# First gate and up weights interleaved by k tile, a row factor by an all-ones product, and one weight unit landing in a place of its own

## The chip, the cores and the metric

The kernel runs on one core of one Trainium2 chip. The metric is device time in microseconds of one execution. Before the change, three runs took 1002.99 to 1003.37 us, median 1003.11.

## The reference

One hybrid decoder layer on 512 tokens of width 1024, in float32: a half-step SwiGLU FFN, a mixer of three head groups (gated DeltaNet, block-sparse attention, cross-attention into 256 memory tokens), and a second half-step FFN. The part that the change touches:

```python
def rms_norm(x, gain, eps=1e-6):
    return x * rsqrt(mean(x * x, axis=-1) + eps) * gain

def swiglu_ffn(x, gain, w_gate, w_up, w_down):          # D_MODEL 1024, D_FF 2816
    h = rms_norm(x, gain)
    return (silu(h @ w_gate) * (h @ w_up)) @ w_down

x = x + 0.5 * swiglu_ffn(x, ffn1_norm, ffn1_w_gate, ffn1_w_up, ffn1_w_down)
...
k, v = split(rms_norm(mem, mem_norm) @ w_mem_kv)        # the memory products, 256 tokens
```

## The kernel before

Activations lie transposed: 128 partitions by 8 k tiles by 512 tokens. Each float32 operand is split into a high part (a rounded copy, type fp32r) and a low part (the remainder), and each product is three matmuls: high by high, high by low, low by high (`split_product`, L1916). A weight unit is 128 x 2048 values (1 MB): SyncE (SP) issues its transfer into one of two `raw` places, ScalarE (ACT) copies the high part into a ring of three `whi` places, and GpSimd (POOL) or VectorE (DVE) subtracts to make `wlo`. TensorE (PE) uses a unit when its low part is done. All queues are written out by hand, instruction by instruction, and tied by semaphores; no scheduler reorders them.

The row factor r = rsqrt(mean of squares) isn't applied to x ahead of the first products. They run on x times the gain, and `gate_scale` (L1241) multiplies the gate tile by r afterwards; `hidden` then multiplies SiLU(gate) by r once more (L1249) and by the up tile (L1253).

The program opens so. SP brings unit 0 (first 256 gate columns, all 8 k tiles) and x in four pieces each, two k tiles at a time (`PIECES`), then unit 1 (the up columns), the memory tokens, unit 2 and 3 (`w_mem_kv`) and the constants. PE runs 28 products on zeros (L2092), then `first_pair` for unit 0 (banks 0 and 1) and for unit 1 (banks 2 and 3), then `x_stats(0)` (sums of squares as four one-column products, L1930), then `mem_keys_values`, with `x_spread(0)` (L1947, the factor spread over the partitions by four small products) after its second k tile. On DVE, `x_stat` makes the sums, computes the factor on 128 x 4 values, and copies the spread factor to `rbc` (L1143). After that come `gate_scale`, `ablo` (L1371), the sums of the memory squares (`mem_sums`, L1199 to L1201), the `cv` copies and a reduction (L1376, L1377), and the first hidden tiles. `normalize` (L1269) and two sums for the later fast products (`t_total`, L1287) follow, then the first residual additions (`ffn_add`, L1363).

PE's second gate and up units (units 4 and 5, with POOL's first low parts, L485) follow the memory products, and then the first down unit (unit 6). PE may overwrite the up bank with unit 5's product only when DVE has made the first hidden tile (`h_done`), and the fifth output tile of the down unit only when DVE has added the first to x (`x_added`).

Stage 2, the norm ahead of the second FFN, already has another way, `x_stat_wide`: a product with an all-ones matrix leaves the sum of squares in every partition, and DVE computes the factor on 128 x 512 values.

Of the kernel before, what the change touches and what calls it, by code (L numbers as in the profile page):

```python
# [11 lines left out]
P = 128  # L12
# [15 lines left out]
U_FIRST, U_MEM = 0, 2  # L28
PIECES = [0, 2, 4, 6, 8]
NP = len(PIECES) - 1  # L30
U_IN = 10
# [37 lines left out]
def build(nc, stream, fast_stream, x_in, mem_in, ab_in, small_in, const_in, out):  # L69
    with ExitStack() as ctx:  # L70
# [96 lines left out]
        gbuf, _, nxt = place("gbuf", [P, 2, T], at=mid)  # L167
        hhi, _, nxt = place("hhi", [P, 4, T], F32R, at=nxt)
# [17 lines left out]
        sum2_hi, sum2_lo, ones_r = (place(f"sum2_{i}", [P, T], F32R, at=nxt2 - (KD - i) * T * 4)[0] for i in (1, 2, 7))  # L186
# [74 lines left out]

        def raw_of(f, g):

            return raw_down[f][:] if g == 2 else raw[:, g, :]
# [28 lines left out]
        def gcol(n, h, c):  # L293
# [3 lines left out]
        cst_in, masks_in, small_sem, ab_sem, out_done = (  # L297
            sem(n) for n in ("cst_in", "masks_in", "small_sem", "ab_sem", "out_done"))
        mem_sems = [sem(f"mem_in{i}") for i in range(2)]
        w0_in = [sem(f"w0_in{i}") for i in range(NP - 1)]  # L300
        half_in = [sem(f"half_in{i}") for i in range(3)]
# [84 lines left out]

        def in_bank(q):

            return q % 4 if q < 12 else q % 2 if q < 23 else 1
# [17 lines left out]
        def _(sp):  # L407
            def part(u, c0, c1, done):
                sp.dma_start(raw[:, u % RAW, c0:c1], stream[u:u + 1, :, c0:c1].rearrange("o p n -> (o p) n")
                             ).then_inc(done, 16)  # L410

            sp.dma_start(small[:], small_in).then_inc(small_sem, 16)
            for i in range(NP):
                k0, k1 = PIECES[i], PIECES[i + 1]
                part(0, 256 * k0, 256 * k1, w0_in[i] if i < NP - 1 else raw_in[0])
                sp.dma_start(x[:, k0:k1, :], x_in[:, k0:k1, :]).then_inc(x_sem[i], 16)
            part(1, 0, 1024, half_in[0])
            part(1, 1024, 2048, raw_in[1])
# [3 lines left out]
            part(2, 0, 1024, half_in[1])  # L422
# [4 lines left out]
            part(3, 0, 1024, half_in[2])  # L427
# [4 lines left out]
            def unit(u):  # L432
                sp.dma_start(raw[:, u % RAW, :], stream[u:u + 1, :, :].rearrange("o p n -> (o p) n")
                             ).then_inc(raw_in[u % RAW], 16)
# [24 lines left out]

            for u in range(EARLY, U_IN):  # L460
                sp.wait_ge(w_lo, u + 1 - RAW)
                unit(u)
# [15 lines left out]
        def _(pool):  # L478
            def split(u):
# [3 lines left out]
                for c0 in range(0, 2048, 2048 // parts):  # L483
                    c1 = c0 + 2048 // parts
                    ins = nc.gpsimd.tensor_tensor(wlo[:, u % RING, c0:c1], raw[:, u % RAW, c0:c1],  # L485
# [56 lines left out]
            pool.wait_ge(masks_in, 16)  # L542
# [26 lines left out]
        def _(act):  # L569
            A = nc.scalar  # L570

            def weight_hi(u):
# [8 lines left out]
                A.activation(whi[:, u % RING, :], raw[:, u % RAW, :], ACT.Copy).then_inc(w_hi, 1)  # L581

            def sqrt(n, width, c0=0):

                act.wait_ge(mean_ready, n + 1)
                A.activation(root[:, c0:c0 + width], msq_[:, c0:c0 + width], ACT.Sqrt).then_inc(root_ready, 1)

# [10 lines left out]
            def part_hi(u, c0, c1, landed, count, done):  # L598
                act.wait_ge(landed, count)
                A.activation(whi[:, u % RING, c0:c1], raw[:, u % RAW, c0:c1], ACT.Copy).then_inc(done, 1)  # L600
# [7 lines left out]
            for i in range(NP):  # L608
                k0, k1 = PIECES[i], PIECES[i + 1]
                if i < NP - 1:  # L610
                    part_hi(0, 256 * k0, 256 * k1, w0_in[i], 16, piece_hi)
                else:
                    part_hi(0, 256 * k0, 256 * k1, raw_in[0], 16, w_hi)
# [3 lines left out]
                for d in range(k0, k1):  # L617
                    x_high(0, S_G1, d)
            part_hi(1, 0, 1024, half_in[0], 16, piece_hi)
            part_hi(1, 1024, 2048, raw_in[1], 16, w_hi)  # L620
            A.activation(gain_qk[:, 0:1], col(S_MQ), ACT.Copy, scale=col(S_MK)).then_inc(gain_ready, 1)
            A.activation(gain_qk[:, 1:2], col(S_CQ), ACT.Copy, scale=col(S_CK)).then_inc(gain_ready, 1)
            for d in range(KD):
                x_square(0, d)
# [4 lines left out]
            part_hi(2, 0, 1024, half_in[1], 16, piece_hi)  # L629
            part_hi(2, 1024, 2048, raw_in[0], 32, w_hi)  # L630
            act.wait_ge(w_used, 1)
# [2202 lines left out]
```

## Time and profile before

| | us |
|---|---|
| median of three runs | 1003.11 |
| the profiled execution | 1002.87 |
| its span | 1001.1 |
| TensorE (PE) busy | 994.9 (99%) |
| VectorE (DVE) busy | 688.7 (69%) |
| GpSimd (POOL) busy | 505.1 (50%) |
| ScalarE (ACT) busy | 440.0 (44%) |

The chain of work that ended last is PE for 92% of the span, half of it the 128 x 512 products of L1916. Busy matmul time is modelled, and matmuls overlap, so the spacing of their starts tells more than their length. Times below are counted from the start of the span. In a timeline a row gives start, length (of the whole group, where it has a count), engine, line, operation, output from inputs, form, count, and in brackets the engine's idle time just before and what ended it.

### The profile page before, as it was taken

The numbers are of one execution on the slowest core, as the hardware profiler recorded it, in microseconds if no ns is written. First come the engines' busy times: TensorE is split into PE (matmuls) and PEld (weight loads), VectorE is DVE, ScalarE is ACT, GpSimd is POOL, SyncE is SP. The second block draws the span as 40 slices with busy tenths as digits, with TensorE's granted clock in tenths as the row PEclk, the third lists the DMA queues.
The fourth block names the chain that finished last, engine by engine and source line by source line (L and its number), as shares of the span: only waits on it lengthen the run. The fifth ranks groups of instructions, "written<-read, shape, count | busy, mean of one in ns | idle before, by whom it ended". The sixth has DMA issues, their size and how long they took to land.

```text
span 1001.1 us, 16467 instructions
## 1 busy us (share of the span) xinstructions
PE 994.9 (99%) x6826; PEld 876.2 (88%) x6826; DVE 688.7 (69%) x1084; ACT 440.0 (44%) x645; POOL 505.1 (50%) x289
## 2 busy tenths in 40 slices
PE   9999999999999999999999999999999999999998
PEld 7888999999999988788878788888899999999997
DVE  5896986766666486863547883687688776667745
ACT  7542543344433462444356664534244244443341
POOL 0364866667566433543252201635576675756741
PEclk9999999999999999999999999999999999999999
DMA  8332223331233212321221001223302332123312
GB/s 331 127 127 84 85 84 127 127 126 51 82 121 127 99 71 85 122 89 43 85 69 61 2 3 43 95 89 112 126 32 96 127 127 104 65 85 127 127 43 84
DMA packets 15770, 95.32 MB, mean 95 GB/s; under 512 B 2000, under 2 KB 2128, under 8 KB 5456
## 3 DMA queue, kind: packets, MB, share of 16 engines
q1 hardware_dynamic: 15696, 94.27, 26.4%
q8 instruction: 54, 0.88, 0.4%
q14 instruction: 20, 0.16, 0.0%
HBM read 92.16 MB, written 2.10 MB: 94 GB/s over the span
## 4 chain that ended last, share of the span: by engine, by line
PE 92%; DVE 3%; DMA 1%; ACT 1%; POOL 1%; SPq 0%; issue 0%; DVEq 0%; POOLq 0%
PE bank L1916 50%; PE bank L2044 32%; DMA raw<-stream 1%; POOL wlo L485 1%; PE bank L2336 1%; PE bank L2340 1%; PE bank L2450 1%; PE bank L2384 1%; PE bank L2362 1%; PE bank L2422 0%; PE bank L2439 0%; ACT sqx L606 0%; PE bank L2406 0%; PE bank L2396 0%; ACT whi L581 0%
## 5 line engine op out<-in xcount | busy, mean ns | idle before, releaser
L485 POOL TENSOR_TENSOR wlo<-raw,whi 128x1024 fp32r<-128x1024 f32 (+1 forms) x44 | 148.3, 3387 | 215.2 <-ACT whi L581 198.4
L2044 PE MATMUL bank<-t_ffn_hi,wlo 128*128 128x256 f32 x896 | 253.6, 283 | 0.0
L2044 PE MATMUL bank<-t_ffn_lo,whi 128*128 128x256 f32 x896 | 253.6, 283 | 0.0
L2044 PE MATMUL bank<-t_ffn_hi,whi 128*128 128x256 f32 x896 | 253.5, 283 | 0.0
L502 POOL TENSOR_TENSOR wlo<-sums,whi 128x512 fp32r<-128x512 f32 x128 | 170.4, 1354 | 120.3 <-ACT whi L695 120.1
L502 POOL TENSOR_TENSOR wlo<-raw,whi 128x512 fp32r<-128x512 f32 x96 | 158.7, 1667 | 39.3 <-ACT whi L695 39.3
L2044 PEld LDWEIGHTS bank<-t_ffn_lo,whi 128*128 128x128 f32 x896 | 172.0, 192 | 0.6
L2044 PEld LDWEIGHTS bank<-t_ffn_hi,whi 128*128 128x128 f32 x896 | 172.0, 192 | 0.6
L1916 PE MATMUL bank<-ahi,whi 128*128 128x512 f32 x432 | 171.2, 396 | 1.0 <-POOL wlo L485 1.0
L2044 PEld LDWEIGHTS bank<-t_ffn_hi,wlo 128*128 128x128 f32 x896 | 172.0, 192 | 0.0
L1916 PE MATMUL bank<-ahi,wlo 128*128 128x512 f32 x432 | 168.4, 390 | 0.0
L1916 PE MATMUL bank<-alo,whi 128*128 128x512 f32 x432 | 168.2, 389 | 0.0
L1363 DVE SCALAR_TENSOR_TENSOR x<-bank,x 128x512 f32<-128x512 f32 x176 | 117.1, 685 | 45.3 <-PE bank L1916 45.2
L1916 PE MATMUL bank<-hhi,whi 128*128 128x512 f32 x352 | 137.1, 390 | 0.0
L1916 PE MATMUL bank<-hlo,whi 128*128 128x512 f32 x352 | 137.1, 390 | 0.0
L1916 PE MATMUL bank<-hhi,wlo 128*128 128x512 f32 x352 | 136.9, 389 | 0.0
L695 ACT ACTIVATE whi<-sums 128x512 fp32r<-128x512 f32 (+2 forms) x72 | 68.4, 961 | 89.4 <-DVE sums L1308 65.6
L1916 PEld LDWEIGHTS bank<-ahi,whi 128*128 128x128 f32 x432 | 81.1, 188 | 20.8 <-POOL wlo L485 1.9
L1916 PEld LDWEIGHTS bank<-ahi,wlo 128*128 128x128 f32 x432 | 81.1, 188 | 17.4
L1916 PEld LDWEIGHTS bank<-alo,whi 128*128 128x128 f32 x432 | 81.2, 188 | 15.9
L695 ACT ACTIVATE whi<-raw 128x512 fp32r<-128x512 f32 (+1 forms) x64 | 54.0, 844 | 82.8 <-PE bank L2044 50.9
L1916 PEld LDWEIGHTS bank<-hhi,wlo 128*128 128x128 f32 x352 | 66.1, 188 | 13.8
(312 smaller groups left out, 1408.2 us busy)
## 6 DMA issues: line engine op xcount, KB each, us to landing
raw<-fast_in SPq DMA_DIRECT2D x32, 1024.0 KB, 4.9
raw<-stream SPq DMA_DIRECT2D x30, 1024.0 KB, 4.9
raw_down<-fast_in SPq DMA_DIRECT2D x18, 1024.0 KB, 7.0
raw<-stream SPq DMA_DIRECT2D x6, 512.0 KB, 6.3
x<-x_in SPq DMA_DIRECT2D x4, 512.0 KB, 6.9
out<-x SPq DMA_DIRECT2D x8, 256.0 KB, 2.0
raw<-stream SPq DMA_DIRECT2D x4, 256.0 KB, 6.1
memx<-mem_in SPq DMA_DIRECT2D x2, 512.0 KB, 10.6
```

The costliest lines, as they stand in the source:

```text
L485: ins = nc.gpsimd.tensor_tensor(wlo[:, u % RING, c0:c1], raw[:, u % RAW, c0:c1], whi[:, u % RING, c0:c1].bitcast(F32), ALU.subtract)
L502: nc.gpsimd.tensor_tensor(in_ring(wlo, ring_at, n), whole[:, PIECE * at:PIECE * (at + 1)], in_ring(whi, ring_at, n).bitcast(F32), ALU.subt ...
L695: A.activation(in_ring(whi, ring_at, m), whole[:, c0:c0 + m], ACT.Copy).then_inc(f_hi, m // PIECE)
L1363: V.scalar_tensor_tensor(out=x[:, d, :], in0=psum[4 + d % 4][:], scalar=0.5, in1=x[:, d, :], op0=ALU.mult, op1=ALU.add).then_inc(x_added, 1)
L1916: ins = E.matmul(dst, a, b, start=(n == 0 and i == 0), stop=(n == last and i == 2))
L2044: ins = E.matmul(psum[bank][:, HALF * h:HALF * (h + 1)], a, b[:, k, :], start=start and k == 0 and m == 0, stop=k == K2 - 1 and m == 2, sk ...
L2336: E.matmul(psum[Y_BANKS[r]][half[e], y_out(j, q)], bm[pair][half[r], j, 2 * q + e, :], x[half[r], j, 2 * q + e, :], start=True, stop=True)
L2340: i = E.transpose(psum[T_BANK][:, M * j + P * q:M * j + P * q + P], x[:, j, 2 * q:2 * q + 2, :].rearrange("p h t -> p (h t)"), ident)
L2362: i = E.matmul(psum[Y_BANKS[e]][half[r], s_out(j, q)], ty[pair][half[e], j, turned(q, r)], ty[pair][half[e], j, product(q, r)], start=True ...
L2384: E.matmul(psum[SCORE_BANKS[e]][:, 0:M], cq[half[e], t, cs], ck[half[e], t, :], start=True, stop=True).then_inc(s_ps, 1)
L2450: i = E.matmul(psum[TURN_BANKS[0]][half[e], 0:P], mv[:, b, v:v + DH], ptr[p % 2][:, e, b, :], start=(b == 0), stop=(b == n - 1))
```

## The change

- **Opening.** Units 0 and 1 are laid out anew on the host: each holds four k tiles, with 256 gate and 256 up columns for each (`both`, `PAIR`). Pieces are now of 1, 1, 2, 2 and 2 k tiles, weights and x in turn. `first_pair` runs k tile by k tile over all four banks. 16 products on zeros stand ahead of it instead of 28. ACT squares x between the pieces.
- **Row factor.** Stage 0 uses `x_stat_wide`, with places of its own for the sums. The all-ones product (`x_sums`, two matmuls of 512 columns) stands ahead of the fifth k tile of the memory products; the four one-column products and the four spreading products go. DVE makes unit 2's and 3's low parts ahead of the last sum. As `x_stat_wide` leaves another value in the bank, `ffn(0)` copies `rbc` there, as `ffn(1)` did.
- **First gate bank.** ACT copies the first two gate tiles out of banks 0 and 1 (`gate_out`), `gate_scale` reads those copies, and PE's second gate unit waits for the copies instead of for `gate_scale`.
- **Unit 4.** It lands in `raw_gate`, over the place of `hhi`, and its transfer waits for unit 2's high part (before: for unit 2's low part). ACT's first `hhi` copy waits until POOL has read it. The last table transfers share one semaphore and stand behind unit 4 on SP.

```diff
-PIECES = [0, 2, 4, 6, 8]
+PIECES = [0, 1, 2, 4, 6, 8]
...
+        raw_gate, _, _ = place("raw_gate", [P, 2048], at=nxt)
...
+        def raw_unit(u):
+            return raw_gate[:] if u == EARLY else raw[:, u % RAW, :]
... (SP)
-            sp.dma_start(abr[:], ab_in).then_inc(ab_sem, 16)
-            sp.dma_start(cst[:, C_LEV:C_SEL], const_in[:, C_LEV:C_SEL]).then_inc(masks_in, 16)
+            sp.wait_ge(w_hi, U_MEM + 1)
+            unit(EARLY)
+            sp.dma_start(abr[:], ab_in).then_inc(tables_in, 16)
+            sp.dma_start(cst[:, C_LEV:C_SEL], const_in[:, C_LEV:C_SEL]).then_inc(tables_in, 16)
... (ACT)
+            for a in range(2):
+                act.wait_ge(gate_done, a + 1)
+                A.activation(gbuf[:, a, :], psum[a][:], ACT.Copy).then_inc(gate_out, 1)
             A.activation(memsq[:, :, :], memx[:, :, :], ACT.Square).then_inc(mem_sq, 1)
...
-            sqrt(0, NC_)
-            weight_hi(4)
+            weight_hi(EARLY)
+            wide_root(0, 0)
... (ACT, hidden_high)
+                    if f == 0 and unit == 0 and a == 0:
+                        act.wait_ge(w_lo, EARLY + 1)
... (DVE, x_stat_wide)
                 link(V.tensor_tensor(sq[:, 0:2, :], sq[:, 0:2, :], sq[:, 2:4, :], ALU.add))
+                if stage == 0:
+                    mem_low(0, 4)
+                    part_lo(2, 0, 1024, piece_hi, NP - 1, piece_lo)
+                    part_lo(2, 1024, 2048, w_hi, 3, w_lo)
+                    part_lo(3, 0, 1024, piece_hi, NP, piece_lo)
+                    part_lo(3, 1024, 2048, w_hi, 4, w_lo)
                 link(V.tensor_tensor(wide, sq[:, 0, :], sq[:, 1, :], ALU.add))
... (DVE, gate_scale)
-                    V.tensor_tensor(gbuf[:, a, :], psum[a][:], rbc[:], ALU.mult).then_inc(gate_scaled, 1)
+                    product = psum[a]
+                    if n == 0:
+                        dve.wait_ge(gate_out, a + 1)
+                        product = gbuf[:, a, :]
+                    V.tensor_tensor(gbuf[:, a, :], product[:], rbc[:], ALU.mult).then_inc(gate_scaled, 1)
... (DVE, ffn)
-                else:
-                    link(V.tensor_copy(psum[R_BANKS[f]][:], rbc[:]))
+                link(V.tensor_copy(psum[R_BANKS[f]][:], rbc[:]))
... (DVE)
-            x_stat(0, 0)
+            x_stat_wide(0, 0)
... (PE, mem_keys_values)
+                    if k == 4:
+                        pe.wait_ge(cst_in, 32)
+                        x_sums(0)
-                    if k == 2:
-                        x_spread(0)
... (PE, first_pair)
-                    for a in range(2):
-                        i = split_product(psum[bank + a][:], wparts(u, k, a * P, P, 256),
+                    for bank in range(4):
+                        i = split_product(psum[bank][:], wparts(k // 4, k % 4, bank * P, P, PAIR),
... (PE, ffn)
-                    for _ in range(28):
-                        E.matmul(psum[7][:], warm[:, 0:P], warm[:], start=True, stop=True)
-                    first_pair(U_FIRST, 0, gate_done)
-                    first_pair(U_FIRST + 1, 2, up_done)
-                    pe.wait_ge(cst_in, 32)
-                    x_stats(0)
+                    for _ in range(16):
+                        E.matmul(psum[4][:], warm[:, 0:P], warm[:], start=True, stop=True)
+                    first_pair()
                     mem_keys_values()
```

SP at the program's start, before (rows: line, transfer, partitions x elements):

```order
L412 DMA small<-small_in 128x93
L409 DMA raw<-stream 128x512
L416 DMA x<-x_in 128x1024
L409 DMA raw<-stream 128x512
L416 DMA x<-x_in 128x1024
```

and changed:

```order
L430 DMA small<-small_in 128x93
L423 DMA raw<-stream 128x512
L435 DMA x<-x_in 128x512
L423 DMA raw<-stream 128x512
L435 DMA x<-x_in 128x512
```

The first two x transfers carry one k tile each (512 values per partition) instead of two; the first weight transfers keep their size and now hold one k tile of gate and up columns.

PE at the end of the first pair and the start of the memory products, before (`sqx` are the squares of x; the row with x4 is `x_stats`):

```order
L1916 MATMUL bank<-ahi,wlo 128x512
L1930 MATMUL bank<-cst,sqx 128x1 x4
L1916 MATMUL bank<-whi,memhi 128x512
L1916 MATMUL bank<-whi,memlo 128x512
L1916 MATMUL bank<-wlo,memhi 128x512
```

and changed, at the boundary of the memory products' fourth and fifth k tile (`sum_7` is the all-ones matrix, `sum_1` and `sum_2` the high and low part of the sums):

```order
L1942 MATMUL bank<-wlo,memhi 128x512
L1966 MATMUL bank<-sum_1_130,sum_7_134 128x512
L1966 MATMUL bank<-sum_2_132,sum_7_134 128x512
L1942 MATMUL bank<-whi,memhi 128x512
L1942 MATMUL bank<-whi,memlo 128x512
```

The statistic's products moved from ahead of the memory products to half way through them, and there are two, of 512 columns.

DVE from the finished factor to the first hidden tile, before (`ablo` and `memsq` belong to the mixer's inputs, `cv` and `rmk` to the memory's values and keys):

```order
L1143 COPY rbc<-bank 128x512
L1241 TENSOR_TENSOR gbuf<-bank,rbc 128x512 x2
L1371 TENSOR_TENSOR ablo<-abr,abhi 128x264
L1199 TENSOR_TENSOR memsq<-memsq 128x1024
L1200 TENSOR_TENSOR memsq<-memsq 128x512
L1201 TENSOR_TENSOR msum<-memsq 128x256
L1376 COPY cv<-bank 128x256 x2
L1377 TENSOR_REDUCE rmk<-mksq 128x8
L1249 TENSOR_TENSOR gbuf<-gbuf,bank 128x512 x2
L1253 TENSOR_TENSOR gbuf<-bank,gbuf 128x512 x2
```

and changed:

```order
L1192 SCALAR_TENSOR_TENSOR rbc<-bank,sqx 128x512
L1268 TENSOR_TENSOR gbuf<-gbuf,rbc 128x512 x2
L1398 TENSOR_TENSOR ablo<-abr,abhi 128x264
L1222 TENSOR_TENSOR memsq<-memsq 128x1024
L1223 TENSOR_TENSOR memsq<-memsq 128x512
L1224 TENSOR_TENSOR msum<-memsq 128x256
L1403 COPY cv<-bank 128x256 x2
L1404 TENSOR_REDUCE rmk<-mksq 128x8
L1406 COPY bank<-rbc 128x512
L1276 TENSOR_TENSOR gbuf<-gbuf,bank 128x512 x2
L1280 TENSOR_TENSOR gbuf<-bank,gbuf 128x512 x2
```

`gate_scale` now reads two SBUF tiles, a copy of the factor to a bank stands ahead of the hidden products, and the rest keeps its order.

## Rows read from the trace of the kernel before

**Rows 1.** The page's slices: granted TensorE clock, tenths of full speed, 40 slices

```profile
PEclk9999999999999999999999999999999999999999
```

**Rows 2.** Waits of PE, whole span: us in total, times, longest

```profile
PE bank L1916 <- POOL wlo L485: 1.0, 2, 0.6
```

**Rows 3.** Timeline of PE, warm-up: all products; then six early ones

```profile
1.31 8.28 PE L2092 MATMUL bank<-warm 128*128 128x512 f32 x28 [1.31 <-POOL warm L490]
...
1.90 2.76 PE L2092 MATMUL bank<-warm 128*128 128x512 f32 x6
```

**Rows 4.** Opening: ACT, DVE timelines; windows (busy PE PEld DVE ACT POOL, clock, DMA, GB/s)

```profile
7.19 1.34 ACT L603 ACTIVATE ahi<-x,small 128x512 fp32r<-128x512 f32 x2 [1.18 <-DMA x<-x_in]
...
8.04 1.41 DVE L1115 SCALAR_TENSOR_TENSOR alo<-x,small,ahi 128x512 fp32r<-128x512 f32 x2 [1.30 <-ACT ahi L603]
...
5.30:6.30 1.00, 1.00 (x6) 0.79 (x5) 0.25 (x1) 0.63 (x1) 0.00 (x0) 1.00 0.97 324
```

**Rows 5.** Timeline of PE: first real product, x_stats, second gate unit

```profile
9.43 0.39 PE L1916 MATMUL bank<-ahi,whi 128*128 128x512 f32 x1
...
31.20 0.95 PE L1930 MATMUL bank<-cst,sqx 128*128 128x1 f32 x8
...
44.55 0.50 PE L1916 MATMUL bank<-ahi,whi 128*128 128x512 f32 x1 [0.43 <-POOL wlo L485]
```

**Rows 6.** Timelines of DVE, ACT and POOL, 21 to 52 us

```profile
21.59 1.67 DVE L1178 SCALAR_TENSOR_TENSOR memlo<-memx,small,memhi 128x256 fp32r<-128x256 f32 x4 [3.78 <-ACT memhi L628]
...
36.68 1.29 DVE L1241 TENSOR_TENSOR gbuf<-bank,rbc 128x512 f32<-128x512 f32 x2
...
38.23 1.22 DVE L1199 TENSOR_TENSOR memsq<-memsq 128x1024 f32<-128x1024 f32 x1
...
42.28 2.50 DVE L1201 TENSOR_TENSOR msum<-memsq 128x256 f32<-128x256 f32 x1
45.47 0.76 DVE L1376 COPY cv<-bank 128x256 f32<-128x256 f32 x2 [0.69 <-ACT mksq L642]
46.14 0.68 DVE L1377 TENSOR_REDUCE rmk<-mksq 128x8 f32<-128x512 f32 x1
49.22 1.28 DVE L1249 TENSOR_TENSOR gbuf<-gbuf,bank 128x512 f32<-128x512 f32 x2 [2.40 <-ACT gbuf L648]
...
36.16 1.92 ACT L581 ACTIVATE whi<-raw 128x2048 fp32r<-128x2048 f32 x1 [3.58 <-DMA raw<-stream]
...
38.23 6.26 POOL L485 TENSOR_TENSOR wlo<-raw,whi 128x1024 fp32r<-128x1024 f32 x2 [36.97 <-ACT whi L581]
47.24 4.78 POOL L485 TENSOR_TENSOR wlo<-raw,whi 128x1024 fp32r<-128x1024 f32 x2 [2.75 <-ACT whi L581]
```

**Rows 7.** Stage 2: timelines of PE and DVE

```profile
664.48 0.39 PE L1940 MATMUL bank<-sum,sum 128*128 128x512 f32 x1
...
665.20 0.70 DVE L1099 TENSOR_SCALAR bank<-bank 128x512 f32<-128x512 f32 x1 [1.81 <-PE bank L1940]
666.64 3.35 DVE L1162 RECIPROCAL sqx<-sqx 128x512 f32<-128x512 f32 x1 [0.73 <-ACT sqx L1081]
...
672.22 1.29 DVE L1241 TENSOR_TENSOR gbuf<-bank,rbc 128x512 f32<-128x512 f32 x2
673.42 0.68 DVE L1380 COPY bank<-rbc 128x512 f32<-128x512 f32 x1
...
675.35 1.28 DVE L1253 TENSOR_TENSOR gbuf<-bank,gbuf 128x512 f32<-128x512 f32 x2
```

**Rows 8.** Timelines of PE, DVE and POOL from the down unit's side, 54 to 69 us

```profile
66.45 0.39 PE L1916 MATMUL bank<-hhi,whi 128*128 128x512 f32 x1
...
59.56 2.94 DVE L1287 TENSOR_TENSOR t_ffn_sum<-xn_ffn 128x1024 f32<-128x1024 f32 x1
...
68.03 0.68 DVE L1363 SCALAR_TENSOR_TENSOR x<-bank,x 128x512 f32<-128x512 f32 x1
...
54.25 10.51 POOL L485 TENSOR_TENSOR wlo<-raw,whi 128x1024 fp32r<-128x1024 f32 x4 [2.23 <-ACT whi L581]
```

More of the change, by code:

```diff
@@ L185, in build @@
         sqx2, _, nxt2 = place("sqx2", [P, KD, T], at=mid + 2 * T * 4)
-        sum2_hi, sum2_lo, ones_r = (place(f"sum2_{i}", [P, T], F32R, at=nxt2 - (KD - i) * T * 4)[0] for i in (1, 2, 7))
+        sum_hi, sum_lo, ones_r = ([place(f"sum{s}_{i}", [P, T], F32R, at=end - (KD - i) * T * 4)[0]
+                                   for s, end in ((0, z_at + KD * T * 4), (2, nxt2))] for i in (1, 2, 7))
         x_hi, x_lo, x_sq = (ahi, ahi, ahi2), (alo, alo, alo2), (sqx, sqx, sqx2)
@@ L385, in build, with first_piece @@
         SCAN_BANK, O_BANKS, STAT_BANK = 1, (0, 0, 4, 4), 6
+        def first_piece(i):
+            k0, k1, u = PIECES[i], PIECES[i + 1], PIECES[i] // 4
+            c0 = PAIR * (k0 - 4 * u)
+            return u, c0, c0 + PAIR * (k1 - k0), i - sum(e < i for e in ENDS)
         def in_bank(q):
@@ L421, in _ @@
             sp.wait_ge(w_lo, 1)
-            part(2, 0, 1024, half_in[1])
+            part(2, 0, 1024, half_in[0])
             part(2, 1024, 2048, raw_in[0])
@@ L458, in ffn_units @@
                              ).then_inc(fast_in[2], 16)
-            for u in range(EARLY, U_IN):
+            for u in range(EARLY + 1, U_IN):
                 sp.wait_ge(w_lo, u + 1 - RAW)
@@ L1931, in x_stats @@
                                  start=True, stop=True)
-                    if c == 0 and stage > 0:
+                    if c == 0:
                         i.then_inc(w_used, 1)
@@ L1939, in x_sums @@
                 for e in range(2):
-                    i = E.matmul(psum[STAT_BANKS[stage][0]][:], ones_r[:, 0:P],
-                                 (sum2_hi, sum2_lo)[e][:], start=(e == 0),
+                    i = E.matmul(psum[STAT_BANKS[stage][0]][:], ones_r[stage // 2][:, 0:P],
+                                 (sum_hi, sum_lo)[e][stage // 2][:], start=(e == 0),
                                  stop=(e == 1))
@@ L1958, in x_spread @@
             def x_spread(stage):
-                pe.wait_ge(rtm_ready, stage + 1)
+                pe.wait_ge(rtm_ready, 1)
                 for c in range(NC_):
@@ L2119, in ffn @@
                     for a in range(2):
-                        up_tile(v, a, a, gate_done, (gate_scaled, done - 1 + a), a == 0, stage)
+                        up_tile(v, a, a, gate_done, (gate_out, 1 + a) if f == 0 and n == 1 else
+                                (gate_scaled, done - 1 + a), a == 0, stage)
                     pe.wait_ge(w_lo, v + 2)
@@ L2801 @@
     first = ffn_units(a["ffn1_w_gate"][0], a["ffn1_w_up"][0], a["ffn1_w_down"][0])
-    units = first[:2] + [w_kv[DH * 8 * i:DH * 8 * (i + 1)].reshape(4, P, 2 * M).transpose(1, 0, 2).reshape(P, 8 * M)
+    both = np.stack([w.reshape(P, KD, 256) for w in first[:2]], axis=2).reshape(P, 2, 2048)
+    units = [both[:, 0], both[:, 1]] + [w_kv[DH * 8 * i:DH * 8 * (i + 1)].reshape(4, P, 2 * M).transpose(1, 0, 2).reshape(P, 8 * M)
                          for i in range(2)] + first[2:]
```

142 lines of the change are left out of this document (67 added, 75 removed).

## The prediction

> **What bounds the kernel now.** I read the page's slices first: TensorE's granted clock stands at its upper level, 2.4 GHz, in every slice [rows 1]. Then the list of who waited for whom, TensorE alone: after its first start it waited 1.0 us for GpSimd's low parts, in two places [rows 2], and there is nothing else of size. So the span is a chain of matrix products, and an edit pays only if products go away, or start earlier without a new wait behind them. The rest is timelines, engine by engine, of the first 75 us, where the diff acts. What to see there: the warm-up products [rows 3], the arrival of the first operands [rows 4], the two small-product groups of the row factor and the wait of 0.43 us at 44.55 [rows 5], and VectorE's path from the row factor to the first hidden tile [rows 6]. Stage 2, late in the same program, already computes its row factor by the all-ones product, so the new VectorE code has a price in this trace [rows 7]. Last, the queue from there to the first residual addition [rows 8].
>
> **Part 1, the earlier start.** 28 warm-up products run from 1.31 us to the first real one at 9.43 [rows 3, 5]. At the start they are 0.426 us apart (six in 2.76 us, one lasting 0.63), later 0.227. With the first step of 0.6, the 8.12 us are seven steps of 0.427 and twenty of 0.227. Sixteen warm-ups therefore end at 1.31 + 0.6 + 7 x 0.427 + 8 x 0.227 = 6.7 us, and then the operands decide. Now the first x piece has two k tiles (512 KB) and ScalarE waits for it until 7.19 [rows 4]; DMA moves 324 GB/s just then, so one k tile (256 KB) lands 0.8 us earlier, and ScalarE starts at 6.4. From there to VectorE's first low part being done are 0.85 + 0.7 us [rows 4], and 0.06 to TensorE: **the first real product starts at 8.0** instead of 9.43. Bounds: 7.6 (x lands right behind the weights) and 8.6 (half the saving). Later pieces are no limit: one k tile now feeds 12 products, 2.72 us, where ScalarE and VectorE need two or three 512-column instructions of about 0.7 us each [rows 4]. The 96 products keep 21.77 us (9.43 to 31.20, 0.2268 each [rows 5]), with four banks in turn instead of two, and end at 29.8.
>
> **Part 2, the row factor.** From 31.20 to the second gate unit at 44.55 are 13.35 us [rows 5]: 48 memory products (10.89), the two groups of small products with their slow follow-ups, and the wait of 0.43. In their place come two products of 512 columns, 0.45 us. If no operand is late, this takes 11.34 us and the second gate unit starts at 29.8 + 11.3 = **41.1, 3.4 us earlier**. Is an operand late? VectorE must have the sums by 35.2. It sat idle 3.78 us before the memory low parts at 21.59 [rows 6]; the order puts the sums of squares in that hole, and the added work before the all-ones product (two low parts of unit 3 of 1024 columns, 1.22 each like the first mem sum, and a high and a low sum at 0.7 each) is 3.8 us. So the sums come near 32, with 3 us to spare. On SP, unit 4 and the tables now stand behind unit 2's high part; before, unit 4 stood behind the low part, a step later, and ScalarE waited 3.58 us for it until 36.16 [rows 6]. On ScalarE the new wait for the first gate tiles holds memsq, abhi and unit 4's high part: the second gate tile is complete at 28.5, two copies of 0.67 end at 29.3, two instructions of 2048 columns take 1.92 each [rows 6], abhi under 0.67: 33.8. GpSimd needs 4.78 to 6.26 us [rows 6] and is done by 40.1. The wait of 0.43 is gone, and the step is hidden under the memory products. The other end: were unit 4 as late as before, GpSimd would end at 44.5 again and TensorE would lose 3.4 us here, and as much less at 52 (part 3).
>
> **Part 3, what the factor's new form costs VectorE.** This decides. Stage 2 has the same code: first all-ones product 664.48, mean 665.20, factor used at 672.22 [rows 7]. That is 7.74 us, of which the reciprocal of 512 columns is 3.35; before, small columns did it. The all-ones product here stands at k tile 4 of the memory products, 29.8 + 5.4 = 35.2, so the factor is used at 42.95. Gate scaling and ablo take 1.55 (36.68 to 38.23 [rows 6]): the three mem sums start at 44.5. Before, GpSimd started a pair of low parts at 38.23, the very moment these sums did, and both ran long: sums 6.55 us (38.23 to 44.78) though the first took 1.22 alone, GpSimd 6.26 instead of 4.78 [rows 6]. Which pair meets them now? GpSimd's pair for unit 5 started 3.12 us after TensorE's last memory product (44.12 to 47.24 [rows 5, 6]); that product now drains at 41.27, so the pair starts at 44.4. **The meeting repeats**, and the sums end at 51.05. Then cv copies and reduction, 1.35 (45.47 to 46.82 [rows 6]) and, new for this stage, the copy of the factor to PSUM, with the hidden products up to the first: 2.62 (673.42 to 676.04 [rows 7]). First hidden tile at 55.05.
>
> TensorE wants it before it may overwrite the up bank. Two units take 21.90 us (44.55 to 66.45 [rows 5, 8]), so it gets there at 41.1 + 10.95 = 52.1 and **waits 3.0 us, to 55.1**. Before, it came at 55.5, without a wait. Of 3.4 us, 0.4 remain.
>
> **Part 4, the queue behind.** VectorE starts the hidden products at 53.16 instead of 49.22, 3.94 us late. From there to the first residual addition at 68.03 it is busy throughout [rows 8], GpSimd's four low parts (54.25 to 64.76) hang on the same hidden tile through ScalarE, and two sums met them (the first took 2.94 for 1024 columns); all shift together. The addition ends at 68.71 + 3.94 = 72.65. TensorE needs it for the fifth output tile of the down unit: before at 66.45 + 24 x 0.2268 = 71.89, now wanted at 55.1 + 10.95 + 5.44 = 71.5, started at 72.7. **A second wait, 1.2 us; TensorE is then 0.8 us behind the old time.** The next additions take 0.68 us each and an output tile 1.36 (six products), so there is no third wait and VectorE catches up. Bounds of this term: no wait if the two sums miss GpSimd (the first alone is then 1.7 us shorter, 1.22), 2.9 if a third instruction loses 1.7.
>
> **Sum.** The profiled execution took 1002.87, span 1001.1; the median of the runs is 1003.11. Saved: start 1.43, small products and wait 2.01. Spent: waits 3.0 and 1.2. Net 0.8 us longer: 1003.7 on the profiled execution, **1003.9 on the median**.
>
> **Rivals.** (a) *The sums and GpSimd do not meet.* Then the three sums take about 2.3 us (1.22 and shares of it), the hidden tile is there at 50.8, before 52.1, nothing queues, and all 3.4 us stay: 999.7. Against it: both starts are tied to the same products, and 44.4 and 44.5 would have to come apart by over 2 us. (b) *The first wait comes, the second does not*: 1002.7. (c) *Slower: the clock.* TensorE's longest wait in this trace is 0.6 us [rows 2], so what one of 3.0 us (or 1.3 us behind the warm-ups) does to the clock is not shown. At the lower level, 1.2 GHz, a product takes 0.427 instead of 0.227, 0.2 us lost each [rows 3]. The first six fall into the wait of 1.2 us that would follow anyway; as many as at the opening (eight) give 1004.3; from about 13 on it is slower by over 2 us, and sixteen give 1005.9. The Trainium skill, "TensorE: Matmul & The Clock Gate", section "Why this matters for your kernels", speaks for (c): it wants no idle gaps of this order between bursts, since the clock falls back to half. No row here shows a fall. (d) *The first x tile lands no earlier*: 1.4 us more, 1005.3.
>
> **Chances.** Forecast 0.55, (b) 0.17, (a) 0.12, (c) with many slow products 0.12, (d) 0.04. A measurement tells about 0.2% (2.0 us) from no change. Faster by more is only (a): 0.12. Slower by more: (c) and (d), 0.16. Within: 0.72. The range has to hold the forecast and (b) with the bounds of start and second wait, and (c) in its milder part: 1002.0 to 1005.5; outside are (a) and the worst of (c).
>
> **What would show it.** Right: first real product near 8.0, second gate unit near 41, then a TensorE wait of about 3 us at 52 released by VectorE's hidden product, the mem sums at 2.5 to 3.3 us each beside GpSimd, a wait near 71.5 released by the residual addition, granted clock at the upper level throughout. Wrong: mem sums under 1.3 us each; no wait at 52; products 0.427 apart after it; an all-ones product waiting for its sums; a wait for GpSimd's unit 4 or 5.

## The result, and the profile after

The changed kernel takes 1006.77 us (median of seven executions, 1003.97 to 1007.79), the kernel before 1003.09 beside it: a ratio of 1.0034, 95% interval 1.0024 to 1.0043. It is **slower by 3.7 us**, where 0.8 us was forecast, and outside the range. The execution whose trace was taken is the fastest of the seven, 1003.97 us with a span of 1002.2 (called the lucky execution below); five of the other six took 1006.6 to 1007.8 and one 1005.55. So there are two questions: whether the trace goes the way that the prediction described, and why the median lies 2.8 us above the time of that trace. One execution in this document, of `both_t1late`, took 2515.93 us for a cause that wasn't found, and stands in no median or ratio below.

The first is quickly answered. VectorE (DVE), GpSimd (POOL) and TensorE (PE) of the changed kernel in that trace, columns as in [rows 6]:

```profile
33.03 1.67 DVE L1204 SCALAR_TENSOR_TENSOR memlo<-memx,small,memhi 128x256 fp32r<-128x256 f32 x4
35.51 0.70 DVE L1123 TENSOR_SCALAR bank<-bank 128x512 f32<-128x512 f32 x1 [0.81 <-PE bank L1966]
36.94 3.35 DVE L1188 RECIPROCAL sqx<-sqx 128x512 f32<-128x512 f32 x1 [0.73 <-ACT sqx L606]
...
42.52 1.29 DVE L1268 TENSOR_TENSOR gbuf<-gbuf,rbc 128x512 f32<-128x512 f32 x2
...
44.08 3.42 DVE L1222 TENSOR_TENSOR memsq<-memsq 128x1024 f32<-128x1024 f32 x1
47.54 2.77 DVE L1223 TENSOR_TENSOR memsq<-memsq 128x512 f32<-128x512 f32 x1
50.34 0.42 DVE L1224 TENSOR_TENSOR msum<-memsq 128x256 f32<-128x256 f32 x1
...
53.99 1.29 DVE L1280 TENSOR_TENSOR gbuf<-bank,gbuf 128x512 f32<-128x512 f32 x2
```

```profile
34.75 4.76 POOL L500 TENSOR_TENSOR wlo<-raw_gate,whi 128x1024 fp32r<-128x1024 f32 x2 [33.49 <-ACT whi L596]
43.97 5.79 POOL L500 TENSOR_TENSOR wlo<-raw,whi 128x1024 fp32r<-128x1024 f32 x2 [4.46 <-ACT whi L596]
```

```profile
7.30 0.47 PE L1942 MATMUL bank<-ahi,whi 128*128 128x512 f32 x1 [0.72 <-DVE alo L1139]
...
40.68 0.39 PE L1942 MATMUL bank<-ahi,whi 128*128 128x512 f32 x1
...
54.82 0.47 PE L1942 MATMUL bank<-ahi,whi 128*128 128x512 f32 x1 [3.10 <-DVE gbuf L1280]
```

The reader is to see the first real product at 7.30 (before 9.43, [rows 5]), the second gate unit at 40.68 (before 44.55), and the memory sums at 44.08 beside unit 5's pair of low parts, where the three take 6.7 us (the first two 3.42 and 2.77); in [rows 6] the three took 6.55. The first hidden tiles stand at 53.99, and TensorE waits 3.10 us for the first of them. Up to this wait it is the chain that was forecast, nearly to the digit; what follows the wait isn't (Part 4 below).

The second question: the same kernel was traced again, as `again` below.

### The profile page after: what moved, and what is told of

Same layout as the page of the kernel before. It is cut to its first block, busy times and chain, and to the rows that moved or that the text cites. A ratio compares the mean times of both kernels' runs of the same rounds, so it can differ in the third digit from the quotient of the medians.

```text
span 1002.2 us, 16423 instructions
## 1 busy us (share of the span) xinstructions
PE 992.6 (99%) x6800; PEld 873.6 (87%) x6800; DVE 698.6 (70%) x1086; ACT 441.1 (44%) x646; POOL 505.0 (50%) x289
## 4 chain that ended last, share of the span: by engine, by line
PE 94%; DVE 4%; ACT 1%; issue 1%; POOL 0%; DMA 0%; SPq 0%; DVEq 0%; ACTq 0%
PE bank L1942 52%; PE bank L2071 32%; PE bank L2357 1%; PE bank L2361 1%; PE bank L2471 1%; PE bank L2405 1%; PE bank L2383 1%; PE bank L2443 0%; POOL wlo L500 0%; PE bank L2460 0%; PE bank L2427 0%; PE bank L2417 0%; PE bank L2307 0%; PE bank L2526 0%; DMA raw<-stream 0%
## 5 line engine op out<-in xcount | busy, mean ns | idle before, releaser
L500 POOL TENSOR_TENSOR wlo<-raw,whi 128x1024 fp32r<-128x1024 f32 (+1 forms) x42 | 143.8, 3441 | 184.9 <-ACT whi L596 168.2
```

What stands on the lines that cost most here:

```text
L500: ins = nc.gpsimd.tensor_tensor(wlo[:, u % RING, c0:c1], raw_unit(u)[:, c0:c1], whi[:, u % RING, c0:c1].bitcast(F32), ALU.subtract)
```

## The experiments

The first four were planned before the cause of the difference was known. Theory A in their expectations knows only the second of the two meetings found below, and the times that it gave for `fill13`, `poolwaits` and `sumslater` were missed by 1.5, 4.4 and over 4 us.

**again**: the changed kernel, unaltered.

> The changed kernel once more, unaltered, for a second profile: the profiled execution of 1003.97 us shows TensorE's clock at its lower level for 3.4 us right behind the wait of 3.1 us for the first hidden tile, and the other executions are 1.6 to 3.8 us longer at a mean granted clock of 0.996 instead of 0.998. Theory A (the wait for the hidden tile lets the clock fall, and in most executions for longer than in the profiled one): the new profile has the same waits to within 0.2 us and its time is longer in step with the time at the lower level, 0.2 us for each product at 0.427 us. Rival B (the executions differ by when transfers land): a longer execution has a later first product, a later row factor or another wait, at the same time at the lower level. Rival C (the gap of 0.7 us behind the warm-up products is what lets the clock fall): the lower level stands before 50 us.

Measured: 1006.67 us (1003.67 to 1007.64), ratio 1.0029 (1.0016 to 1.0042). Its trace is of an execution of 1006.69 us, so of the usual kind by its time. (Its mean granted clock is 0.998; in most others of this length it is 0.996, so those stood longer at the lower level, and no trace of one was taken.) VectorE there, with GpSimd's two pairs of low parts:

```profile
33.35 5.94 DVE L1204 SCALAR_TENSOR_TENSOR memlo<-memx,small,memhi 128x256 fp32r<-128x256 f32 x4
39.21 0.69 DVE L1123 TENSOR_SCALAR bank<-bank 128x512 f32<-128x512 f32 x1
...
46.21 4.67 DVE L1268 TENSOR_TENSOR gbuf<-gbuf,rbc 128x512 f32<-128x512 f32 x2
...
51.15 1.21 DVE L1222 TENSOR_TENSOR memsq<-memsq 128x1024 f32<-128x1024 f32 x1
...
56.77 1.28 DVE L1280 TENSOR_TENSOR gbuf<-bank,gbuf 128x512 f32<-128x512 f32 x2
```

```profile
33.68 4.92 POOL L500 TENSOR_TENSOR wlo<-raw_gate,whi 128x1024 fp32r<-128x1024 f32 x2 [32.43 <-ACT whi L596]
45.13 5.20 POOL L500 TENSOR_TENSOR wlo<-raw,whi 128x1024 fp32r<-128x1024 f32 x2 [6.52 <-ACT whi L596]
```

The last four memory low parts take 5.94 us instead of 1.67, because GpSimd's pair for unit 4 starts at 33.68, in the middle of them. The mean, next on VectorE, starts at 39.21 instead of 35.51. The later meeting then strikes the gate scaling (4.67 instead of 1.29) instead of the memory sums, and the hidden tiles come at 56.77, 2.8 us later than above. TensorE's waits in the two traces (us in total, times, longest), first `again`, then the lucky execution:

```profile
PE bank L1942 <- DVE gbuf L1280: 4.7, 1, 4.7
...
PE bank L1942 <- DVE memlo L1204: 0.6, 1, 0.6
PE bank L1942 <- POOL wlo L500: 0.6, 1, 0.6
```

```profile
PE bank L1942 <- DVE gbuf L1280: 3.1, 1, 3.1
...
PE bank L1942 <- DVE alo L1139: 0.7, 1, 0.7
PE bank L1942 <- POOL wlo L500: 0.6, 1, 0.6
```

Why one execution escapes is seen on ScalarE (ACT), first in the lucky one, then in `again`:

```profile
32.37 0.42 ACT L659 ACTIVATE abhi<-abr 128x264 fp32r<-128x264 f32 x1 [1.65 <-DMA cst<-const_in]
32.70 1.90 ACT L596 ACTIVATE whi<-raw_gate 128x2048 fp32r<-128x2048 f32 x1
```

```profile
31.30 0.43 ACT L659 ACTIVATE abhi<-abr 128x264 fp32r<-128x264 f32 x1 [0.26 <-DMA cst<-const_in]
31.63 1.90 ACT L596 ACTIVATE whi<-raw_gate 128x2048 fp32r<-128x2048 f32 x1
```

This is rival B of the expectation: the tables land 1.07 us later in the lucky execution. Unit 4's high part stands behind them on ScalarE, and GpSimd behind that: its pair starts at 34.75, when the memory low parts (33.03 + 1.67 = 34.70) are just done. VectorE's own start, 0.3 us earlier than in `again`, is needed too: from 33.35 the low parts would end at 35.02, behind the pair's start. In the traces of `fill13`, `poolwaits` and `sumslater`, as in `again`, the pair starts 0.3 to 0.8 us behind the first of these low parts, in the lucky one 1.7. So here a later transfer goes with a faster program. That the pair's start decides is so far an argument from traces; `u4waits` tests it. The new theory has **two meetings**: unit 4's pair with the memory low parts, in most executions, and unit 5's pair with the memory sums (or the gate scaling).

**fill13**: 13 products of no use on TensorE, ahead of the first up unit, to keep it busy through its wait (they start when the row factor is ready); nothing is left out.

> Thirteen extra products of 512 columns into a bank that nobody reads (work added, nothing left out) stand on TensorE's queue between the second gate unit and the up unit that waits for the first hidden tile: 13 x 0.227 = 2.95 us of the wait of 3.1 us are filled with products, while VectorE, ScalarE, GpSimd and the transfers do what they did. Theory A: the granted clock stays at its upper level throughout; the wait for the first residual addition, which the slow products covered in the profiled execution, comes back with about 1 us; the median is 1004.0 us (1003.6 to 1004.4) with all executions within 0.6 us. Rivals B and C (transfers, or the gap behind the warm-up products): median 1006.5 to 1007 us and a spread of 2 us or more, as without the filling.

```diff
+                    if f == 0 and n == 1:
+                        pe.wait_ge(r_ready, 1)
+                        for _ in range(13):
+                            E.matmul(psum[6][:], ahi[:, 0, 0:P], ahi[:, 0, :], start=True, stop=True)
                     for a in range(2):
                         up_tile(v + 1, a, 2 + a, up_done, ...)
```

Measured: 1005.45 us (1004.17 to 1006.43), ratio 1.0023 (1.0014 to 1.0033). Behind the wait the products stand 0.23 us apart, and the mean granted clock is 0.999 or 1.0 in all ten executions; 1.2 us of the 3.4 that the change costs are gone. TensorE's waits, and then the product that ends the first of them, here and in `again`:

```profile
PE bank L1942 <- DVE gbuf L1280: 1.8, 1, 1.8
...
PE bank L1942 <- DVE x L1390: 0.9, 1, 0.9
```

```profile
56.80 0.47 PE L1942 MATMUL bank<-ahi,whi 128*128 128x512 f32 x1 [1.78 <-DVE gbuf L1280]
```

```profile
57.60 0.55 PE L1942 MATMUL bank<-ahi,whi 128*128 128x512 f32 x1 [4.72 <-DVE gbuf L1280]
```

The wait for the hidden tile is 1.8 us instead of 4.7 (13 products fill 2.95), and a wait of 0.9 us for the first residual addition appears, which the slow products hid in `again`. The slow products cost 1.7 us there (nine products from 57.60 to 61.32, 3.72 us, where 0.227 us each make 2.04), and the new wait takes part of that back. How much is left isn't clean here. TensorE goes on 0.8 us earlier than in `again`, ahead of any slow product, because VectorE's low parts began 0.9 us earlier in this execution (32.43 for 33.35), and this is part of the 1.2 us between the two traces. The memory low parts take 5.99 us here too, and the time stays 2.2 us above the kernel before, with the clock up: the clock isn't the main cause.

**poolwaits**: GpSimd starts unit 5's pair only behind the memory sums.

> GpSimd's low parts of unit 5 wait until VectorE has made the three memory sums; nothing else is altered. Theory A (the sums meet that pair on VectorE and GpSimd, which alone makes the hidden tile late): the sums take 2.3 us together instead of 6.7, the hidden tile is done near 50.4, GpSimd's pair runs 46.4 to 51.2 and is just in time, TensorE waits 0.3 us at most at 51, the clock stays at its upper level, the residual addition costs up to 0.7 us, and the median is 999.3 us (998.8 to 1000.2). Rival D (the wide factor alone, 7.7 us from its product to its use, is what makes the tile late): the sums get shorter, but the wait stays above 2 us and the time above 1002.

```diff
             for u in range(EARLY, U_IN):
+                if u == EARLY + 1:
+                    pool.wait_ge(mem_sum, 1)
                 split(u)
```

Measured: 1003.67 us (1002.26 to 1004.01), ratio 1.0001 (0.9991 to 1.0010). Its trace is of the fastest of ten executions, 1002.26 us. Four of the ten have a mean granted clock of 1.0 and take 1002.26 to 1002.98 us, the other six 0.998 and 1003.55 to 1004.01. In the trace the meeting with unit 5's pair is gone: gate scaling takes 1.29 us, the first memory sum 1.22. Here too the low parts of the first meeting are long, and the factor late, so that GpSimd, which now waits for the sums behind it, is late in its turn:

```profile
32.50 5.94 DVE L1206 SCALAR_TENSOR_TENSOR memlo<-memx,small,memhi 128x256 fp32r<-128x256 f32 x4
```

```profile
PE bank L1944 <- POOL wlo L500: 2.7, 2, 2.1
```

**sumslater**: the memory sums behind the first hidden tiles instead of ahead of them.

> VectorE makes the three memory sums behind the first two hidden products instead of ahead of the cv copies; nothing else is altered. Theory A: the hidden tile is done near 47.5, no wait at 52, the clock stays at its upper level; but the sums now delay normalize and everything up to the first residual addition, and meet GpSimd's next pair, so the wait for that addition is 1 to 3 us: 1000 to 1002.3 us. Rival D (the wide factor alone): the wait at 52 stays above 1 us. Rival E (the lag behind the hidden tile does not reach TensorE): no wait for the addition, 999.0 us.

```diff
-                    mem_sums()
...
                 hidden(f, 0)
+                if f == 0:
+                    mem_sums()
```

Measured: 1006.37 us (1005.74 to 1006.62), ratio 1.0028 (1.0016 to 1.0040). No gain: the low parts take 5.95 us, and unit 5's pair meets the gate scaling instead of the sums (4.27 us), as it does in `again`. Moving the victim of a meeting gives GpSimd another one: the pair runs from 44.22 to 49.4, and the gate scaling starts at 45.71, within it. TensorE waits 2.4 us for the hidden tile and 2.8 us, later, for a low part of GpSimd's.

The next four put the two meetings to the test, `u4waits` and `bothwaits` by waits on GpSimd alone.

**u4waits**: unit 4's pair waits for the eight memory low parts.

> One edit to the changed kernel: GpSimd starts unit 4's pair of low parts only when VectorE has made all eight memory low parts. Nothing is left out. New theory (two meetings): in the usual execution the pair starts near 33.4 us, while VectorE's last four memory low parts run from 33; they take 5.9 us instead of 1.7, the factor comes 3.7 us later, and that is what the median has over the profiled 1003.97. Then here the memory low parts take 1.7 us in every execution, the mean starts near 35.5, TensorE waits about 3.1 us at 52 for the hidden product (the second meeting, mem sums with unit 5's pair, is left in), and the median is about 1004.0 us with a narrow spread. Rival (the recorded forecast's terms were only mis-sized, and the extra 3 us come from the lower clock behind the wait): nothing changes in the clock, so the median stays near 1006.7.

```diff
             for u in range(EARLY, U_IN):
+                if u == EARLY:
+                    pool.wait_ge(mem_lo, 8)
                 split(u)
```

Measured: 1004.07 us (1003.64 to 1005.29), ratio 1.0010 (1.0001 to 1.0019). That is the 1004.0 of the two meetings, 2.6 us under `again`, and the rest of the trace is the lucky execution's:

```profile
33.31 1.66 DVE L1206 SCALAR_TENSOR_TENSOR memlo<-memx,small,memhi 128x256 fp32r<-128x256 f32 x4
35.83 0.70 DVE L1125 TENSOR_SCALAR bank<-bank 128x512 f32<-128x512 f32 x1 [0.86 <-PE bank L1968]
...
44.39 3.42 DVE L1224 TENSOR_TENSOR memsq<-memsq 128x1024 f32<-128x1024 f32 x1
```

The clock still falls behind the wait of 3.1 us in this trace, so the fall as such isn't what the usual execution loses over the lucky one; `u4fill` below sizes its share. In three of the ten executions the mean granted clock is 1.0, and they take 1003.64 to 1003.93 us.

**bothwaits**: both waits.

> Two edits to the changed kernel, both on GpSimd: unit 4's pair waits for the eight memory low parts, unit 5's pair for the sum of the memory squares. Nothing is left out. Two meetings theory: no VectorE instruction of the factor's path meets GpSimd, so the hidden tile is there at about 51, before TensorE wants it at 51.5 to 52; no wait over 0.9 us at 52, no residual wait, clock at the upper level throughout, and all of the saving stays: 1003.2 - 2.1 (start) - 2.0 (small products and their wait) = about 999.2 us. Rival (GpSimd's later unit 5 takes the place of the wait): unit 5's pair ends at 46.4 + 4.8 = 51.2, and any us by which it is later than that is a TensorE wait for it; with 2 us of that, 1001.2 us.

```diff
             for u in range(EARLY, U_IN):
+                if u == EARLY:
+                    pool.wait_ge(mem_lo, 8)
+                if u == EARLY + 1:
+                    pool.wait_ge(mem_sum, 1)
                 split(u)
```

Measured: 999.94 us (999.55 to 999.97), ratio 0.9967 (0.9955 to 0.9980), **faster than both kernels**. No VectorE instruction of the chain is long any more, and GpSimd's wait costs nothing, since its pair for unit 5 ends at 51.35, before TensorE wants it:

```profile
44.11 1.22 DVE L1226 TENSOR_TENSOR memsq<-memsq 128x1024 f32<-128x1024 f32 x1
45.36 0.69 DVE L1227 TENSOR_TENSOR memsq<-memsq 128x512 f32<-128x512 f32 x1
...
49.74 1.29 DVE L1284 TENSOR_TENSOR gbuf<-bank,gbuf 128x512 f32<-128x512 f32 x2
```

```profile
34.72 4.75 POOL L500 TENSOR_TENSOR wlo<-raw_gate,whi 128x1024 fp32r<-128x1024 f32 x2 [33.47 <-DVE memlo L1208]
46.59 4.76 POOL L500 TENSOR_TENSOR wlo<-raw,whi 128x1024 fp32r<-128x1024 f32 x2 [7.12 <-DVE msum L1228]
```

Neither wait 1006.7, one of them 1004.1 or 1003.7, both 999.9. The first alone gives 2.6 us, the second alone 3.0, the two together 6.7: more than the sum. In the traces each alone still leaves TensorE a long wait, 3.1 us for the hidden tile in `u4waits` and 2.1 us for GpSimd in `poolwaits`.

**u4fill**: `u4waits` with the 13 products of `fill13`; its edit is the two diffs above together.

> u4waits and beside it 13 products of no use (2.95 us) on TensorE between the second gate unit and the up unit, which fill the wait at 52 and so keep the clock up; nothing is left out. Against u4waits this isolates what the lower clock costs. Two meetings theory with covered slow products: ten slow products cost 2.0 us, but the residual addition that follows isn't ready earlier, so they fall into a wait of 1.2 to 2 us that comes here instead: within 0.6 us of u4waits, near 1004.0. Rival (the clock costs its full 2 us): 2 us below u4waits, near 1002.0.

Measured: 1003.65 us (1003.47 to 1003.86), ratio 1.0005 (0.9996 to 1.0014), 0.42 us under `u4waits`. Here the lower clock costs little, as a wait for the residual addition stands where the slow products stood:

```profile
PE bank L1944 <- DVE x L1392: 0.9, 1, 0.9
```

The slow products of `u4waits` are eight, not ten: from 55.13 to 58.62 they take 3.49 us, where 0.227 us each make 1.82, so 1.7 us more. The four runs together also size the first meeting. With the 13 products, so with the clock up, it costs 1.8 us (1005.45 in `fill13` against 1003.65); without them 2.6 us (1006.67 against 1004.07). So some 0.8 of the 2.6 us go with the lower clock.

**warm28** and **both28**: 28 warm-up products again, in the changed kernel and in `bothwaits`.

> The changed kernel with 28 warm-up products as before, in place of 16: TensorE's first real product goes back to about 9.4 us (from 7.3 to 7.9), nothing else is touched or left out. If the start counts in full (term 1 of the sum), the time grows by 1.5 to 2.1 us, to 1008.2 to 1008.8. If the path through VectorE to the hidden tile sets the time (its squares, memory low parts and the factor hang on transfers and ScalarE, not on the first products), the later start only shortens the wait at 52: within 0.6 us of the changed kernel, near 1006.7. Two meetings theory says the second.

> bothwaits with 28 warm-up products instead of 16, so that the first real product goes from 7.5 back to about 9.7 us; nothing else is changed or left out. It repeats warm28 without either meeting, since in warm28 the first meeting went away together with the early start. If the start counts in full: 999.9 + 2.2 = about 1002.1 us. Rival (VectorE's path sets the time here too, and the late start is taken up by TensorE's small waits at the start and at 68.7 us, 0.8 us each): 1000.3 to 1001.2 us.

```diff
-                    for _ in range(16):
+                    for _ in range(28):
```

Measured: `warm28` 1006.22 us (1005.90 to 1006.76), `both28` 1001.50 us (1000.90 to 1001.96). The first has the number that was expected for a start that doesn't count, and for another reason. In its trace ScalarE waits for the later products ahead of unit 4's high part, GpSimd's pair comes at 34.95, and the memory low parts, done at 33.9, miss it. So it has to be held against `u4waits`, which has no first meeting either: traces of 1005.90 and 1004.25 us, first products at 9.69 and 7.88, so 1.65 us for a start 1.81 us later (the medians are 2.15 us apart). The cleaner pair is `both28` and `bothwaits`: 1001.96 and 999.97 us for first products at 10.11 and 7.50. Of the 2.61 us, 2.0 are seen in the time, and 0.5 come out of TensorE's wait for the first residual addition, which is 0.2 us instead of 0.7 by the list of waits. By the medians the two are 1.56 us apart. So the start counts, less what a later wait takes up.

**before_warm16**: the kernel before with 16 warm-up products.

> The kernel before with 16 warm-up products instead of 28; nothing is left out. It tells how much of the earlier start is due to the warm-ups and how much to the smaller pieces. In the trace of before the first x low part is done at about 8.7 us, so with the pieces of before the first product can start at 8.8 instead of 9.43: about 0.6 us faster, 1002.6 us. Rival (the gap of 2 us behind the warm-ups lowers the clock, some ten products at half speed): 2 us given back, 1004.6 us.

Measured: 1002.52 us (1002.45 to 1003.03), ratio 0.9995 (0.9986 to 1.0005). That is the 0.6 us that were expected, but not clear of noise. Its first product starts at 8.93 instead of 9.43. So fewer warm-ups alone bring the start forward by 0.5 us, and with them the smaller pieces bring another 1.1 to 1.6 (7.30 to 7.88 in the changed kernel). The smaller pieces alone bring nothing: behind 28 warm-ups the first product stands at 9.69 (`warm28`). The 2.4 us that TensorE idles behind the warm-ups leave the clock where it is (last section).

**both_t1late**: `bothwaits`, with one low part behind the first additions.

> bothwaits with one more move: VectorE makes the low part of the first fast operand (t_low of T_1, 3.43 us where it meets GpSimd) behind the first output tiles' additions instead of ahead of them; nothing is left out. In bothwaits TensorE waits 0.8 us at 68.7 for the first residual addition, which stands behind that low part. Expected: that wait goes, 0.8 us faster, about 999.1 us. Rival (the low part meets GpSimd or delays the second hidden tile in its new place): no gain, 999.9 us or up to 1001.

> both_t1late once more, unaltered, for a trace of an undisturbed execution: the median near 999.1 us as before. In the trace TensorE's wait at 68.7 us for the first residual addition (0.8 us in bothwaits) should be gone, since the addition starts 3.4 us earlier than at 68.0; the second hidden tile should be no later than TensorE wants it. Rival: the gain came from elsewhere, and the wait of 0.8 us still stands there.

```diff
                 t_low(f, T_B11)
-                t_low(f, T_1)
...
                 hidden_low(f, 1)
+                t_low(f, T_1)
                 t_low(f, T_3)
```

Measured: 999.09 us (998.99 to 999.19) in four executions, ratio 0.9960 (0.9947 to 0.9974); in `both_t1late2`, from which the trace is, 999.11 us (999.02 to 999.17), ratio 0.9957 (0.9941 to 0.9974). The additions in `bothwaits`, and then here:

```profile
64.64 3.43 DVE L1322 TENSOR_TENSOR t_ffn_lo<-t_ffn_sum,t_ffn_hi 128x1024 fp32r<-128x1024 f32 x1
68.00 2.47 DVE L1394 SCALAR_TENSOR_TENSOR x<-bank,x 128x512 f32<-128x512 f32 x4
```

```profile
65.25 1.21 DVE L1322 TENSOR_TENSOR t_ffn_lo<-xn_ffn,t_ffn_hi 128x1024 fp32r<-128x1024 f32 x1
66.39 2.62 DVE L1394 SCALAR_TENSOR_TENSOR x<-bank,x 128x512 f32<-128x512 f32 x4
```

TensorE's wait at 68.7 is gone, though the addition is only 1.6 us earlier and not 3.4: two sums ahead of it meet GpSimd in their turn. This is the fastest version, 4.2 us under the kernel before.

## Why the prediction was wrong, by its own steps

**Part 1** held, and was a little short. The start was forecast at 8.0 (bounds 7.6 to 8.6) and measured at 7.30 to 7.88, in part below the bounds. It counts in the time for the most part: 1.65 us for 1.81 (`warm28` against `u4waits`), 1.6 to 2.0 for 2.61 (`both28` against `bothwaits`).

**Part 2 is the step that failed**: "the step is hidden under the memory products", at no cost. What it put at nothing, without a reason, is the price that GpSimd's earlier pair for unit 4 has for VectorE. It asked whether GpSimd's unit 4 is done in time for TensorE, and it is. It didn't ask what VectorE does while GpSimd works. Both numbers stand in that paragraph: the sums "come near 32", so the four memory low parts behind them, 1.67 us, run until about 33.7; and unit 4's high part is ready at 33.8, when GpSimd starts. Part 3 lets the same two engines meet ten microseconds later, with rows for it [rows 6], and the same look at this place would have found a margin of 0.1 us, and so the chance of a meeting. Its price in the trace of `again` is 4.3 us on VectorE (5.94 for 1.67). The mean is 3.7 us later than in the lucky execution and 3.4 later than in `u4waits`, and the hidden tile 2.5 us later than in `u4waits` (TensorE goes on at 57.60 instead of 55.13), since unit 5's pair then costs the gate scaling 3.4 us where it cost the sums 4.3. In the median that is 2.6 us (1006.67 against 1004.07; some 0.8 of it by the lower clock, `u4fill`), and nearly the whole difference between the forecast 1003.9 and the measured 1006.77.

**Part 3** held for the execution that escapes the first meeting: factor used at 42.52 (forecast 42.95), memory sums at 44.08 (44.5), GpSimd at 43.97 (44.4), TensorE's wait 3.10 (3.0). In the usual execution it starts from a mean 3.7 us too late, and the meeting strikes the gate scaling instead of the sums. "The meeting repeats" is shown by `bothwaits` and `u4waits`: without it the time is 4.1 us less.

**Part 4** held in size, by another way. VectorE's first residual addition started at 71.56 (forecast 71.97, to end at 72.65). TensorE didn't wait for it, because the slow products behind the first wait took up the time (ten products from 55.13 to 59.01, 3.88 us, where 0.227 us each make 2.27: 1.6 us more). This is what rival (c) said of its first six products. A fall with many slow products had been given 0.12, a milder one no chance of its own, and "granted clock at the upper level throughout" stood among the signs of being right. It fell in both traces of the changed kernel. Its net price is 0.4 us where TensorE waits 3.1 us (`u4fill`), which is what rival (c) gave for eight slow products, and some part of 1.2 us where it waits 4.7 (`fill13`).

**Rival (a)**, no meeting at all, gave 999.7 us; with both meetings taken away the chip gives 999.94. The saving of 3.4 us was there, and GpSimd's timing ate it. The profiled execution, at 1003.97 us, agrees with the forecast of 1003.7 by luck, a favourable landing of the tables and slow products in the place of the second wait; one trace alone would have confirmed a sum that lacked a term of 2.6 us.

## What to carry to other kernels

Where two engines hold each other up, an edit that moves either has to be checked at every place where both are busy, for the one engine's next instruction as well as for the deadline of the other's result. If such a meeting is decided by 1 us of a transfer's landing, look at several executions: the spread of times is the first sign. A wait on the engine that has slack, so that the engine on the path goes first, can be worth more than the edit that brought the two together.

## What the runs showed of the hardware

- **Who waits for whom, VectorE and GpSimd.** While GpSimd subtracts two tiles in SBUF (2.4 us for 1024 columns), a VectorE instruction with both inputs in SBUF stands still, and it is the short one that loses most in proportion (0.48 to 2.62 us, where the first memory sum goes from 1.22 to 3.42). In `again` one memory low part takes 2.62 us, where the median of that line is 0.48, beside one low part of GpSimd's:

```profile
33.74 2.62 DVE L1204 SCALAR_TENSOR_TENSOR memlo<-memx,small,memhi 128x256 fp32r<-128x256 f32 x1
...
33.68 2.39 POOL L500 TENSOR_TENSOR wlo<-raw_gate,whi 128x1024 fp32r<-128x1024 f32 x1 [32.43 <-ACT whi L596]
```

  The two instructions shown next, one with an input in SBUF and one in PSUM and one with a single input in SBUF, aren't touched. In `bothwaits` the hidden product below runs from 48.53 and the reciprocal from 36.97, both beside GpSimd, at the lengths that they have without it.

```profile
48.53 1.29 DVE L1280 TENSOR_TENSOR gbuf<-gbuf,bank 128x512 f32<-128x512 f32 x2
...
36.97 3.35 DVE L1192 RECIPROCAL sqx<-sqx 128x512 f32<-128x512 f32 x1 [0.74 <-ACT sqx L610]
```

  The change itself made one more victim: `gate_scale` now reads two SBUF tiles where it read a bank, and takes 4.67 us in `again`, 1.29 in the lucky execution. The Trainium skill, "SBUF — State Buffer", section "SBUF: two separate sides", describes a port pair that the two engines share as an exclusive lock for whole instructions, for VectorE with two SBUF inputs; the traces agree, with the 2.62 us.

- **The clock.** The table gives, by windows, busy us (and instructions) of PE, PEld, DVE, ACT and POOL, the granted clock, the DMA share and GB/s. In `again`, behind the wait of 4.72 us, then in the lucky execution, behind one of 3.10:

```profile
57.80:61.30 3.50, 3.50 (x9) 2.71 (x9) 3.40 (x6) 3.50 (x4) 0.70 (x1) 0.51 0.04 9
61.50:64.00 2.50, 2.50 (x12) 2.04 (x12) 2.50 (x5) 1.78 (x2) 2.50 (x2) 1.00 0.00 0
```

```profile
55.50:58.80 3.30, 3.30 (x10) 2.53 (x9) 3.30 (x6) 3.30 (x3) 0.98 (x1) 0.50 0.03 7
```

  At 0.50 (the lower level, 1.2 GHz) products stand 0.43 us apart instead of 0.23 (six steps from 57.95 to 60.51 in `again`); the window of the lucky execution touches ten of them, the first and the last in part. In `sumslater` a wait of 2.83 us is followed by the lower level, one of 2.41 us isn't, and three executions of `u4waits` keep a mean of 1.0; what length of wait it takes is open. In `before_warm16` a wait of 2.36 us, behind sixteen warm-ups, is followed by products at the upper level:

```profile
8.93 0.47 PE L1916 MATMUL bank<-ahi,whi 128*128 128x512 f32 x1 [2.36 <-DVE alo L1115]
...
9.00:12.00 3.00, 3.00 (x14) 2.47 (x15) 2.97 (x5) 2.20 (x5) 0.00 (x0) 1.00 1.03 376
```

- **Slow products can be nearly free.** Where TensorE runs into a second wait anyway, the lower clock mostly fills it: 0.4 us net for eight slow products that take 1.7 us longer (`u4fill` against `u4waits`).
